# Expert down rows asked for by ScalarE on its own DMA queue, gate and up rows by the sync engine on the other

## The chip, the core and the metric

The kernel runs on one core of a Trainium2 chip. A core has five instruction streams: TensorE (PE, matmuls; its weight loads are shown apart as PEld), VectorE (DVE), ScalarE (ACT), GpSimd (POOL) and the sync engine (SP). Streams meet only at semaphores. Data come from device memory (HBM) by DMA: an instruction of one of the streams asks for a transfer, sixteen DMA engines carry it out, and a semaphore says that it has landed. The metric is the time on the device in microseconds (us).

## The reference, cut to what matters

The program is a two-layer decoder trunk. Each layer has three token mixers, a merge, an output projection and a channel mixer. The channel mixer of the second layer is a mixture of experts, and the change lies there alone:

```
logits = (tokens @ router_w)                       # 256 tokens, 8 experts
top_vals, top_idx = lax.top_k(logits, 2)
top_w = softmax(top_vals)
for e in range(8):                                 # w_gate, w_up: 1024 x 3584, w_down: 3584 x 1024
    y = (silu(tokens @ w_gate[e]) * (tokens @ w_up[e])) @ w_down[e]
    out = out + combine[:, e:e+1] * y
out = rmsnorm(x + out, final_norm_g)
```

All is float32, so that the eight experts are 352 MB of weights, each of which is read once in the run of the profile.

## The kernel before, in words

Everything up to line 1185 (both layers' mixers, the dense channel mixer, the routing) is the same in both kernels. Then comes the expert loop. Work is cut into passes: one pass takes one expert and up to 80 (CAP) of the tokens that chose it. The number of passes is found on the chip (`pass_expert`, a small table in SBUF, also says which expert each pass takes). The profile shows eight passes. A pass gathers its tokens into `xgT`, goes through four rounds (NR), and scatters the result into `x`.

A round covers 896 of the 3584 hidden columns, and needs 11 pieces of weights, each with a buffer of its own and no second one:

- eight "hidden" pieces (`hidden_slot(n)`, 128 x 2 x 896 floats): gate rows for even n, up rows for odd n;
- three "down" pieces (`down_slot(n)`): two of 128 x 2 x 1024 floats and one of 128 x 3 x 1024.

TensorE (L1217 to L1302) does in each round `hidden()`, which multiplies by the hidden pieces in order n = 0 to 7 and adds one to `hid_used` when it is through with each; then `down(0)`, which waits for down pieces 0 and 1 at its start, multiplies by them and adds one to `dwn_used`; then `down(1)`, which waits for piece 2, multiplies by it in two halves and adds one to `dwn_mm` after each. All three are the helper `columns_mm`, whose matmuls stand at L639; a round has 448 matmul records for the hidden part (56 for each piece) and 224 for the down part (128 in `down(0)`, 96 in `down(1)`). Between hidden and down, ScalarE takes Silu of the gate half in two parts (L1584, L1587) and VectorE multiplies by the up half (L2023, L2026). After round four, ScalarE copies the sums out of PSUM (`yT`, L1592), TensorE turns them (L1292), ScalarE copies them again (`ye`, L1596), TensorE scatters (L1298), turns the next pass's selection (L1210) and gathers its tokens.

The sync engine asks for all weights, in one queue (q1 in the trace). For each round it runs `later_round` (L2156): eight times "wait until TensorE is through with hidden piece n of the round before, ask for the next" (L2123), then down pieces 0 and 1 behind a wait on `dwn_used`, then piece 2 behind a wait on `dwn_mm` (L2128). Since it takes its instructions in order, the down pieces of a round always stand in the queue behind that round's hidden pieces, which is the order in which TensorE needs them. The last round of a pass asks for the first round of the next pass; two reads of `pass_expert` into a register (L2177, L2179) say from which expert. The first round's pieces of the first pass are asked for earlier, at L2138 to L2150, also by SP.

Of the kernel before, what the change touches and what calls it, by code (L numbers as in the profile page):

```python
# [9 lines left out]
ACT = mybir.ActivationFunctionType  # L10
AX_X = mybir.AxisListType.X

P = 128
# [12 lines left out]
FFD, FFE, NE = 2816, 3584, 8  # L26
# [4 lines left out]
CAP = 80  # L31
MAX_PASSES = 2 * T // CAP + NE
MIN_PASSES = -(-2 * T // CAP)
# [6 lines left out]
FB = 7  # L40
NR = FT // FB
SPLIT = 4
HSLOT = 2 * FB * P
KH = 4
# [23 lines left out]
def build(nc, a, out):  # L68
    ctx = ExitStack()
    with ctx:  # L70
        def sb(name, shape, dt=F32):
            return ctx.enter_context(nc.sbuf_tensor(name, shape, dt))

        def sem(name):
            return ctx.enter_context(nc.semaphore(name))
# [46 lines left out]
        def region(floats, at=None):  # L122
            start = top[0] if at is None else at
            assert start + floats <= ring_floats + arena_floats, (start, floats, ring_floats + arena_floats)
            top[0] = max(top[0], start + floats) if at is None else top[0]
            return pool[:, start:start + floats]
# [8 lines left out]
        def down_slot(n):  # L135

            lo = 2 * KH * HSLOT
            return pool[:, lo + 2 * n * D:lo + min(2 * n + (3 if n == 2 else 2), FB) * D].rearrange("p (f n) -> p f n", n=D)
# [4 lines left out]
        proj, B = banks[:2], banks[2:]  # L143
# [82 lines left out]
        sge = region(FB * CAP).rearrange("p (j n) -> p j n", j=FB)  # L226
# [10 lines left out]
        pass_expert = sb("pass_expert", [1, 32], I32)  # L237
# [14 lines left out]
        hid_loaded, dwn_loaded = slot_loaded[0:2 * KH], slot_loaded[2 * KH:2 * KH + 3]  # L252
        hid_used = sem("hidden_used")
        dwn_used = sem("down_used")
# [184 lines left out]
        he_silu, he_ready, hid_mm, dwn_mm = ff_silu.handle, ff_ready.handle, proj_mm.handle, down_mm.handle  # L439
# [31 lines left out]
        hid_base = DEPTH * proj_mm.per_layer  # L471
        ff_base = ff_ready.per_layer
        down_base = down_mm.per_layer

        block = ctx.enter_context(nc.Block())


        @block.gpsimd
        def _(gp):
# [846 lines left out]
        def _(act):  # L1326
# [8 lines left out]
            A = act.activation  # L1335

            def ln_exp_tables():

                act.preload_act_table_set("natural_log_exp_and_others")
# [237 lines left out]
            act.wait_ge(margin_ready, 1)  # L1577
            A(rs[:, 8:10], rs[:, 4:6], ACT.Exp).then_inc(marg_exp, 1)
            act.wait_ge(passes_ready, 1)
            n_pass = act.value_load(pass_expert[0:1, 0:1], min_val=MIN_PASSES, max_val=MAX_PASSES)  # L1580
            with act.Fori(0, n_pass) as i:
                for r in range(NR):
                    act.wait_ge(hid_mm, i * NR + (hid_base + r + 1))
                    A(sge[:, 0:SPLIT, :], B[2][:, 0:SPLIT * CAP].rearrange("p (f n) -> p f n", f=SPLIT),  # L1584
                      ACT.Silu).then_inc(he_silu, 1)
                    act.wait_ge(hid_used, i * (2 * KH * NR) + (2 * KH * (r + 1)))
                    A(sge[:, SPLIT:FB, :], proj[0][:, 0:(FB - SPLIT) * CAP].rearrange("p (f n) -> p f n", f=FB - SPLIT),  # L1587
                      ACT.Silu).then_inc(he_silu, 1)

                for half in range(2):  # L1590
                    act.wait_ge(dwn_mm, i * (2 * NR) + (down_base + 2 * NR - 1 + half))
                    A(yT[:, 4 * half:4 * half + 4, :], B[4 + half][:, 0:4 * CAP].rearrange("p (k n) -> p k n", k=4),  # L1592
                      ACT.Copy).then_inc(yT_ready, 1)
                for half in range(2):
                    act.wait_ge(ye_mm, i * 2 + (half + 1))
                    A(ye[0:CAP, half * 512:half * 512 + 512], B[2 + half][0:CAP, :], ACT.Copy).then_inc(ye_ready, 1)  # L1596
            ln_exp_tables()
            for t in range(NT):
                act.wait_ge(all_added, t + 1)
# [473 lines left out]
        def _(sp_):  # L2073
# [16 lines left out]
            def load(n):  # L2090

                src, _, s, _, former = loads[n]
                if former is not None:
                    sp_.wait_ge(*freed[former])
                if n == L[0]["ffn_first"]:
                    merge_step.wait(sp_, 0, 12)
                if n >= L[0]["ffn_first"] and former is None and (s + 1) * SLOT > mT_at:
                    xo_mm.wait(sp_, 0, 4)
                sp_.dma_start(weights(n), src).then_inc(slot_loaded[s], 16)
# [18 lines left out]
            def hidden_load(n, e, col):  # L2118

                w = (a["moe_w_gate"], a["moe_w_up"])[n % 2]  # L2120
                rows = slice(n // 2 * 2 * P, (n // 2 + 1) * 2 * P)
                src = w[0, e, rows, col].rearrange("a (k p) n -> p (a k) n", p=P)
                sp_.dma_start(hidden_slot(n), src).then_inc(hid_loaded[n], 16)  # L2123

            def down_load(n, e, rows):

                src = a["moe_w_down"][0, e, rows, :].rearrange("a (f p) n -> p (a f) n", p=P)
                sp_.dma_start(down_slot(n), src).then_inc(dwn_loaded[n], 16)  # L2128

            def down_rows(n):  # L2130
                return 2 * n * P, (3 if n == 2 else 2) * P


            oc_ready.wait(sp_, DEPTH - 1, 4)
            for n in range(RING, MRING):
# [1 line left out]
                    sp_.wait_ge(*freed[slot_last[n]])  # L2137
            for n in range(3):  # L2138
                lo, size = down_rows(n)
                down_load(n, slice(0, 1), slice(lo, lo + size))  # L2140
            clear, fetched = [], []
            for ring in [None] + sorted(range(RING), key=lambda n: slot_last[n]):
                if ring is not None:
# [9 lines left out]
            sp_.wait_ge(passes_ready, 1)  # L2153
            sp_.dma_start(fgain, a["final_norm_g"].partition_broadcast(P)).then_inc(fgain_loaded, 16)

            def later_round(e, col, hid, dwn):  # L2156

                for n in range(2 * KH):
                    sp_.wait_ge(hid_used, hid + (n + 1))
                    hidden_load(n, bass.ds(e, 1), bass.ds(col, FB * P))  # L2160
                for n in range(3):
                    if n < 2:
                        sp_.wait_ge(dwn_used, dwn + 1)
                    else:
                        sp_.wait_ge(dwn_mm, dwn * 2 + (down_base + 2))
                    lo, size = down_rows(n)
                    down_load(n, bass.ds(e, 1), bass.ds(col + lo, size))

            def rest_of_pass(i, e):

                with sp_.Fori(0, NR - 1) as j:
                    later_round(e, j * (FB * P) + FB * P, i * (2 * KH * NR) + j * (2 * KH), i * NR + j)

            more = sp_.value_load(pass_expert[0:1, MAX_PASSES + 1:MAX_PASSES + 2], min_val=MIN_PASSES - 1,
                                  max_val=MAX_PASSES - 1)
            with sp_.Fori(0, more) as i:
                e = sp_.value_load(pass_expert[0:1, bass.ds(i + 1, 1)], min_val=0, max_val=NE - 1)  # L2177
                rest_of_pass(i, e)
                e = sp_.value_load(pass_expert[0:1, bass.ds(i + 2, 1)], min_val=0, max_val=NE - 1)  # L2179
                later_round(e, 0, i * (2 * KH * NR) + (2 * KH * (NR - 1)), i * NR + (NR - 1))  # L2180
            e = sp_.value_load(pass_expert[0:1, bass.ds(more + 1, 1)], min_val=0, max_val=NE - 1)
            rest_of_pass(more, e)
            for t in range(NT):
                sp_.wait_ge(*((fin0_ready, 2), (fin_ready, 1))[t])
# [30 lines left out]
```

## Time and profile before

| | |
|---|---|
| median of 3 runs | 2028.77 us (2024.67 to 2029.76) |
| the profiled execution's own time | 2029.26 us |
| its span, first to last instruction | 2027.5 us |
| mean granted TensorE clock | 0.988 of full speed |
| busy: PE, PEld, DVE, ACT, POOL | 1951.6, 1729.5, 391.8, 273.1, 87.9 us |
| DMA | 482.99 MB |

The span is cut into 40 slices of 50.7 us in the page's second part. The expert loop fills the last 17 of them. A busy PE is not PE at its peak: the ends of matmuls are modelled, and short waits inside a merged run of matmuls may not show. "SPq" is the sync engine's own sequencer, and the duration of a DMA row there is the time that asking took, not the transfer's.

### The profile page before, as it was taken

What the parts mean: (1) busy time and instruction counts of PE and PEld (TensorE: products, weight loads), DVE (VectorE), ACT (ScalarE), POOL (GpSimd) and SP (SyncE); (2) the same over time, 40 slices, a digit from 0 to 9 for tenths busy, and PEclk for the clock granted to TensorE, in tenths of its full rate; (3) what the DMA queues carried; (4) which work ended last, traced back from release to release, by engine and by line L of the source; (5) the groups of instructions that cost most, each with busy time, mean ns of one, the idle gap of its engine ahead of it and who ended that gap; (6) DMA issues with size and microseconds to landing.
All of it is one profiled execution on the core that took longest, in us unless ns stands there. A gap on an engine that the chain in (4) does not pass through costs nothing.

```text
span 2027.5 us, 67804 instructions
## 1 busy us (share of the span) xinstructions
PE 1951.6 (96%) x31726; PEld 1729.5 (85%) x31726; DVE 391.8 (19%) x945; ACT 273.1 (13%) x580; POOL 87.9 (4%) x174
## 2 busy tenths in 40 slices
PE   7999999999999999999999799999999999999998
PEld 7888888888777688888888799999999898989897
DVE  3335331110000133533211301001010101010001
ACT  1323214000000122222310000000000000000001
POOL 4011101000000001011100000000000000000000
PEclk9999999999999999999999799999999999999999
DMA  7413123466443051320337299999999999999996
GB/s 243 125 45 103 44 85 104 146 221 236 145 145 104 22 167 43 104 65 23 125 125 251 102 380 407 407 407 407 407 407 407 407 407 407 407 407 407 407 407 267
DMA packets 214764, 482.99 MB, mean 238 GB/s; under 512 B 11582, under 2 KB 110092, under 8 KB 214668
## 3 DMA queue, kind: packets, MB, share of 16 engines
q1 hardware_dynamic: 214668, 481.54, 63.9%
q8 instruction: 81, 1.33, 0.3%
q14 instruction: 15, 0.12, 0.0%
HBM read 480.46 MB, written 1.05 MB: 237 GB/s over the span
## 4 chain that ended last, share of the span: by engine, by line
PE 84%; DMA 6%; SPq 4%; DVE 3%; ACT 1%; issue 1%; POOL 0%; DVEq 0%; ACTq 0%
PE bank L639 32%; PE bank L626 18%; PE bank L1154 7%; DMA pool<-in_moe_w_down_dram 6%; PE bank L723 5%; PE bank L1081 4%; PE bank L1114 4%; SPq L2123 3%; PE bank L1097 3%; PE bank L687 2%; PE bank L1298 1%; SPq L2128 1%; PE bank L1044 1%; DVE pool L1817 0%; PE bank L1004 0%
## 5 line engine op out<-in xcount | busy, mean ns | idle before, releaser
L639 PE MATMUL bank<-pool 128*64 128x80 f32 x21504 | 760.0, 234 | 31.7 <-DMA pool<-in_moe_w_down_dram 23.9
L639 PEld LDWEIGHTS bank<-pool 128*64 128x64 f32 x21504 | 754.0, 138 | 39.1 <-DMA pool<-in_moe_w_down_dram 26.0
L626 PE MATMUL bank<-hnT,pool 128*128 128x256 f32 x1856 | 427.7, 384 | 0.4 <-DVE pool L1879 0.4
L626 PEld LDWEIGHTS bank<-hnT,pool 128*128 128x128 f32 x1856 | 346.1, 190 | 55.1 <-issue 8.8
L1154 PEld LDWEIGHTS bank<-hnT,pool 128*128 128x128 f32 x640 | 121.6, 190 | 23.4 <-issue 7.7
L1154 PE MATMUL bank<-hnT,pool 128*128 128x256 f32 x640 | 140.7, 379 | 0.0
L2023 DVE TENSOR_TENSOR pool<-pool,bank 128x320 f32<-128x320 f32 x32 | 15.6, 488 | 638.4 <-ACT pool L1584 638.4
L723 PEld LDWEIGHTS bank<-pool 64*64 64x64 f32 x3008 | 94.8, 135 | 17.2 <-issue 11.3
L1584 ACT ACTIVATE pool<-bank 128x320 f32<-128x320 f32 x32 | 14.0, 437 | 690.1 <-PE bank L639 690.1
L723 PE MATMUL bank<-pool 64*64 64x32 f32 (+2 forms) x3008 | 103.4, 221 | 2.6 <-DVE pool L1663 1.6
L564 POOL TENSOR_TENSOR pool<-pool,level_mask 128x256 f32<-128x256 f32 x72 | 51.9, 735 | 773.8 <-DVE pool L1739 493.8
L1081 PE MATMUL bank<-oT,pool 128*128 128x256 f32 x384 | 85.4, 380 | 0.0
L1081 PEld LDWEIGHTS bank<-oT,pool 128*128 128x128 f32 x384 | 72.8, 190 | 10.2 <-issue 0.3
L1114 PE MATMUL bank<-pool 128*128 128x512 f32 x176 | 78.4, 593 | 0.0
L1114 PEld LDWEIGHTS bank<-pool 128*128 128x128 f32 x176 | 33.4, 190 | 35.0 <-issue 30.3
L1097 PE MATMUL bank<-pool 128*128 128x256 f32 x256 | 55.9, 379 | 0.0
L1097 PEld LDWEIGHTS bank<-pool 128*128 128x128 f32 x256 | 48.5, 190 | 6.5
L639 PE MATMUL bank<-hnT,pool 128*64 128x128 f32 x768 | 47.2, 288 | 3.5 <-DVE hnT L1634 3.5
L639 PEld LDWEIGHTS bank<-hnT,pool 128*64 128x64 f32 x768 | 45.8, 146 | 4.8 <-issue 4.8
L1913 DVE TENSOR_TENSOR pool<-pool,bank 128x256 f32<-128x256 f32 x22 | 9.3, 421 | 194.6 <-ACT pool L1562 194.6
L1663 DVE TENSOR_TENSOR pool<-pool,bank 128x128 f32<-128x128 f32 x108 | 26.7, 284 | 92.5 <-PE bank L723 92.5
L2035 DVE TENSOR_TENSOR x<-x,bank 128x512 f32<-128x512 f32 x32 | 22.0, 687 | 97.7 <-PE bank L1298 97.7
(324 smaller groups left out, 1188.4 us busy)
## 6 DMA issues: line engine op xcount, KB each, us to landing
pool<-in_moe_w_up_dram SPq DMA_DIRECT2D x128, 896.0 KB, 16.6
pool<-in_moe_w_gate_dram SPq DMA_DIRECT2D x128, 896.0 KB, 16.5
pool<-in_w_in_dram SPq DMA_DIRECT2D x66, 1024.0 KB, 5.4
pool<-in_moe_w_down_dram SPq DMA_DIRECT2D x64, 1024.0 KB, 16.6
pool<-in_moe_w_down_dram SPq DMA_DIRECT2D x32, 1536.0 KB, 18.6
pool<-in_ffn_w_gate_dram SPq DMA_DIRECT2D x11, 1024.0 KB, 7.6
pool<-in_ffn_w_up_dram SPq DMA_DIRECT2D x11, 1024.0 KB, 5.6
pool<-in_ffn_w_down_dram SPq DMA_DIRECT2D x11, 1024.0 KB, 5.1
```

Of the source, the lines that this page charges most:

```text
L564: ml_ready.by(gp.tensor_tensor(Ml[:, 4 * g:4 * g + 4, :], m_of(g), rep(level_mask[:, b, :], 4), ALU.mult))
L626: ins = mm(ps[:, s * T:(s + 1) * T], w[:, k, (j + s) * P:(j + s + 1) * P], hnT[:, k, :], start=(k == 0), stop=(k == KD - 1))
L639: ins = mm(bank[rows, cs], w[:, rows], rhs, start=start, stop=stop, skip_group_check=True)
L687: ins = mm(ps[:, half * SW:(half + 1) * SW], hnT[:, k, t * P:(t + 1) * P], weights(n)[:, k, :], start=(k == 0), stop=(k == KD - 1))
L723: ins = mm(out(rows), lhs(rows), rhs(rows), start=True, stop=True, skip_group_check=True)
L1081: ins = mm(ps[:, s * T:(s + 1) * T], weights(n)[:, k, (j0 + s) * P:(j0 + s + 1) * P], oT[:, m // 4, k, :], start=(k == 0), stop=(k == GH - 1))
L1097: ins = mm(bank[:, s * SW:(s + 1) * SW], mT[:, k, t * P:(t + 1) * P], weights(n)[:, k, :], start=(k == 0), stop=(k == KD - 1))
L1114: ins = mm(B[2 * t + half][:, :], ffT[:, f, t * P:(t + 1) * P], weights(n)[:, i, half * 512:half * 512 + 512], start=(f == 0), stop=(f == ...
L1154: ins = mm(proj[f % 2][:, s * T:(s + 1) * T], w[:, k, i * P:(i + 1) * P], hnT[:, k, :], start=(k == 0), stop=(k == KD - 1))
L1663: ins = tt(old, old, part(B[2 + g][:, k * T:(k + 1) * T]), ALU.subtract)
L2035: ins = tt(x[:, t, cs], x[:, t, cs], (B[0], B[1], proj[0], proj[1])[t + 2 * half][:, :], ALU.add)
L2123: sp_.dma_start(hidden_slot(n), src).then_inc(hid_loaded[n], 16)
```

## The change

The down pieces of all rounds but the very first are now asked for by ScalarE, whose requests go to another queue than SP's. `down_rows` and `down_load` move to the top of the block and take the queue as an argument. SP's `later_round` keeps the eight hidden pieces. ScalarE's loop, which ran over all passes, now runs over all but the last, as SP's did; it reads the expert's number into a register twice in a pass. In a pass it does: `hidden_round` (the two Silus), then `down_round` for the next round (the same waits, on `dwn_used` and `dwn_mm`, and the same three requests), three times; the fourth `hidden_round`; `outputs` (`yT`); the second read of the table; `rows_out` (`ye`); and only then `down_round` for the next pass's first round.

```
+            def down_round(e, row, used):
+                act.wait_ge(dwn_used, used + 1)
+                for n in range(3):
+                    if n == 2:
+                        act.wait_ge(dwn_mm, used * 2 + (down_base + 2))
+                    lo, size = down_rows(n)
+                    down_load(act, n, bass.ds(e, 1), slice(row + lo, row + lo + size))
...
+            def rounds(i, e):
+                for r in range(NR):
+                    hidden_round(i, r)
+                    if r < NR - 1:
+                        down_round(e, (r + 1) * (FB * P), i * NR + r)
+                outputs(i)
+
+            with act.Fori(0, more) as i:
+                e = act.value_load(pass_expert[0:1, bass.ds(i + 1, 1)], min_val=0, max_val=NE - 1)
+                rounds(i, e)
+                e = act.value_load(pass_expert[0:1, bass.ds(i + 2, 1)], min_val=0, max_val=NE - 1)
+                rows_out(i)
+                down_round(e, 0, i * NR + (NR - 1))
+            e = act.value_load(pass_expert[0:1, bass.ds(more + 1, 1)], min_val=0, max_val=NE - 1)
+            rounds(more, e)
+            rows_out(more)
...
-            def later_round(e, col, hid, dwn):
+            def later_round(e, col, hid):
                 for n in range(2 * KH):
                     sp_.wait_ge(hid_used, hid + (n + 1))
                     hidden_load(n, bass.ds(e, 1), bass.ds(col, FB * P))
-                for n in range(3):
-                    if n < 2:
-                        sp_.wait_ge(dwn_used, dwn + 1)
-                    else:
-                        sp_.wait_ge(dwn_mm, dwn * 2 + (down_base + 2))
-                    lo, size = down_rows(n)
-                    down_load(n, bass.ds(e, 1), bass.ds(col + lo, size))
```

ScalarE at the end of a pass, before. The first pair of rows is `yT`, the second `ye`, the last two close the loop:

```order
L1591 ISA
L1592 ACTIVATE pool<-bank 128x320 [waits down_mm]
L1591 REGISTER_ALU
L1592 ACTIVATE pool<-bank 128x320 [waits down_mm]
L1595 ISA
L1596 ACTIVATE hnT<-bank 80x512 [waits ye_mm]
L1595 REGISTER_ALU
L1596 ACTIVATE hnT<-bank 80x512 [waits ye_mm]
L1581 REGISTER_ALU
L1581 COMPARE_AND_BRANCH
```

Nothing stands between the copies and the next pass. The same place in the changed kernel, from the second `yT` copy on:

```order
L1613 ACTIVATE pool<-bank 128x320 [waits down_mm]
L1633 ISA
L1633 TENSOR_LOAD pass_expert
L1633 ISA x2
L1619 ISA
L1620 ACTIVATE hnT<-bank 80x512 [waits ye_mm]
L1619 REGISTER_ALU
L1620 ACTIVATE hnT<-bank 80x512 [waits ye_mm]
L1593 REGISTER_ALU
L484 ISA [waits down_used]
L484 DMA pool<-in_moe_w_down_dram 128x2x1024
L484 ISA
```

A read of the table now stands ahead of the `ye` copies, and the down requests of the next pass behind them. The sync engine in the second part of its pass loop, before, from the last hidden piece to the end of the pass:

```order
L2123 DMA pool<-in_moe_w_up_dram 128x2x896 [waits hidden_used]
L2163 ISA
L2128 DMA pool<-in_moe_w_down_dram 128x2x1024 [waits down_used]
L2128 ISA [waits down_used]
L2128 DMA pool<-in_moe_w_down_dram 128x2x1024
L2165 ISA
L2128 ISA [waits down_mm]
L2128 DMA pool<-in_moe_w_down_dram 128x3x1024
L2176 REGISTER_ALU
L2176 COMPARE_AND_BRANCH
```

The down requests stood right behind the last hidden request. The same place in the changed kernel:

```order
L2165 DMA pool<-in_moe_w_gate_dram 128x2x896
L2193 REGISTER_ALU
L2165 DMA pool<-in_moe_w_up_dram 128x2x896 [waits hidden_used]
L2203 REGISTER_ALU
L2203 COMPARE_AND_BRANCH
```

SP goes from the last hidden request straight to the next pass. The order on TensorE, VectorE and GpSimd is the same in both.

## Rows read from the trace of the kernel before

**Rows 1.** The page, span in 40 slices: TensorE, DMA share, GB/s

```profile
PE   7999999999999999999999799999999999999998
DMA  7413123466443051320337299999999999999996
GB/s 243 125 45 103 44 85 104 146 221 236 145 145 104 22 167 43 104 65 23 125 125 251 102 380 407 407 407 407 407 407 407 407 407 407 407 407 407 407 407 267
```

**Rows 2.** Windows: from:to, length, busy and count by engine, PEclk, DMA share, GB/s

```profile
1300.00:1400.00 100.00, 96.90 (x2635) 93.20 (x2632) 9.98 (x26) 6.57 (x13) 0.00 (x0) 1.00 1.03 407
...
1600.00:1700.00 100.00, 94.07 (x2541) 90.07 (x2539) 9.98 (x26) 6.57 (x13) 0.00 (x0) 1.00 1.03 407
...
2000.00:2027.50 27.50, 18.41 (x386) 15.33 (x386) 6.66 (x9) 7.99 (x14) 0.00 (x0) 0.95 0.38 150
```

**Rows 3.** The page, DMA issues: op xcount, KB each, us to landing

```profile
pool<-in_moe_w_up_dram SPq DMA_DIRECT2D x128, 896.0 KB, 16.6
...
pool<-in_moe_w_down_dram SPq DMA_DIRECT2D x64, 1024.0 KB, 16.6
pool<-in_moe_w_down_dram SPq DMA_DIRECT2D x32, 1536.0 KB, 18.6
```

**Rows 4.** DMA queues from 1200 to 2000 us: packets, MB, share

```profile
q1 hardware_dynamic: 92374, 325.78, 102.6%
q8 instruction: 1, 0.02, 0.0%
q14 instruction: 2, 0.02, 0.0%
```

**Rows 5.** TensorE's waits from 1200 us on: us in total, times, longest

```profile
PE bank L639 <- DMA pool<-in_moe_w_down_dram: 23.9, 13, 2.1
...
PE bank L639 <- DMA pool<-in_moe_w_up_dram: 3.9, 5, 0.9
```

**Rows 6.** Chain of waits: start us, us, what

```profile
1481.57 62.42 PE bank L639 x1792
```

**Rows 7.** Timeline at the end of a pass: start us, us, engine, line, operation

```profile
1445.72 6.12 SPq L2128 DMA_DIRECT2D pool<-in_moe_w_down_dram  x3
1452.98 2.72 SPq L2123 DMA_DIRECT2D pool<-in_moe_w_gate_dram  x1
...
1464.93 7.97 PE L639 MATMUL bank<-pool 128*64 128x80 f32 x224 [1.87 <-DMA pool<-in_moe_w_down_dram]
...
1472.28 6.81 SPq L2128 DMA_DIRECT2D pool<-in_moe_w_down_dram  x3
...
1472.94 0.44 ACT L1592 ACTIVATE pool<-bank 128x320 f32<-128x320 f32 x1 [1.22 <-PE bank L639]
...
1473.49 1.20 ACT L1596 ACTIVATE hnT<-bank 80x512 f32<-80x512 f32 x2
...
1481.57 28.66 PE L639 MATMUL bank<-pool 128*64 128x80 f32 x819
1485.08 0.38 SPq L2123 DMA_DIRECT2D pool<-in_moe_w_gate_dram  x1
```

**Rows 8.** Timeline of the last round on TensorE

```profile
2000.82 2.99 PE L639 MATMUL bank<-pool 128*64 128x80 f32 x80 [0.92 <-DMA pool<-in_moe_w_up_dram]
...
2005.94 7.97 PE L639 MATMUL bank<-pool 128*64 128x80 f32 x224 [2.13 <-DMA pool<-in_moe_w_down_dram]
```

**Rows 9.** DMA from 1990 to 2027.5 us in 40 slices of 0.94 us

```profile
GB/s 409 405 401 413 401 401 421 394 408 415 415 411 406 402 411 406 415 406 201 61 13 0 0 0 0 0 0 0 0 0 0 0 0 0 0 0 315 406 393 4
```

**Rows 10.** Line 2128 from 1200 us on: request ns min/median/max, landing

```profile
L2128 SPq DMA_DIRECT2D pool<-in_moe_w_down_dram x90: 372/1852/2755, 1209.9 to 1991.1; - x90
...
DMA to landing us min/median/max: 8.9/16.9/19.1
```

**Rows 11.** A request into an idle queue; then DMA from 1140 to 1160 us in slices of 0.5 us

```profile
1157.10 0.34 SPq L2154 DMA_DIRECT2D hnT<-in_final_norm_g_dram  x1
```

```profile
GB/s 409 409 444 409 409 445 409 409 409 172 0 0 0 0 0 0 0 0 0 0 0 0 0 0 0 0 0 0 0 0 0 0 0 0 0 0 180 401 295 123
```

More of the change, by code:

```diff
@@ L475, in build, with down_rows, down_load @@
         block = ctx.enter_context(nc.Block())
+        def down_rows(n):
+            return 2 * n * P, (3 if n == 2 else 2) * P
+        def down_load(queue, n, e, rows):
+            src = a["moe_w_down"][0, e, rows, :].rearrange("a (f p) n -> p (a f) n", p=P)
+            queue.dma_start(down_slot(n), src).then_inc(dwn_loaded[n], 16)
         @block.gpsimd
@@ L1579, in _, with hidden_round, outputs @@
             act.wait_ge(passes_ready, 1)
[L1580 to L1588, printed above, removed]
+            more = act.value_load(pass_expert[0:1, MAX_PASSES + 1:MAX_PASSES + 2], min_val=MIN_PASSES - 1,
+                                  max_val=MAX_PASSES - 1)
+            def down_round(e, row, used):
[5 more added lines that the diff above has]
+                    down_load(act, n, bass.ds(e, 1), slice(row + lo, row + lo + size))
+            def hidden_round(i, r):
+                act.wait_ge(hid_mm, i * NR + (hid_base + r + 1))
+                A(sge[:, 0:SPLIT, :], B[2][:, 0:SPLIT * CAP].rearrange("p (f n) -> p f n", f=SPLIT),
+                  ACT.Silu).then_inc(he_silu, 1)
+                act.wait_ge(hid_used, i * (2 * KH * NR) + (2 * KH * (r + 1)))
+                A(sge[:, SPLIT:FB, :], proj[0][:, 0:(FB - SPLIT) * CAP].rearrange("p (f n) -> p f n", f=FB - SPLIT),
+                  ACT.Silu).then_inc(he_silu, 1)
+            def outputs(i):
                 for half in range(2):
@@ L1593, in _, with rows_out @@
                       ACT.Copy).then_inc(yT_ready, 1)
+            def rows_out(i):
                 for half in range(2):
@@ L2123, in hidden_load @@
                 sp_.dma_start(hidden_slot(n), src).then_inc(hid_loaded[n], 16)
[L2125 to L2131, printed above, removed]
             oc_ready.wait(sp_, DEPTH - 1, 4)
@@ L2139, in _ @@
                 lo, size = down_rows(n)
-                down_load(n, slice(0, 1), slice(lo, lo + size))
+                down_load(sp_, n, slice(0, 1), slice(lo, lo + size))
             clear, fetched = [], []
@@ L2160, in later_round @@
                     hidden_load(n, bass.ds(e, 1), bass.ds(col, FB * P))
-                for n in range(3):
-                    if n < 2:
-                        sp_.wait_ge(dwn_used, dwn + 1)
-                    else:
-                        sp_.wait_ge(dwn_mm, dwn * 2 + (down_base + 2))
-                    lo, size = down_rows(n)
-                    down_load(n, bass.ds(e, 1), bass.ds(col + lo, size))
             def rest_of_pass(i, e):
                 with sp_.Fori(0, NR - 1) as j:
-                    later_round(e, j * (FB * P) + FB * P, i * (2 * KH * NR) + j * (2 * KH), i * NR + j)
+                    later_round(e, j * (FB * P) + FB * P, i * (2 * KH * NR) + j * (2 * KH))
             more = sp_.value_load(pass_expert[0:1, MAX_PASSES + 1:MAX_PASSES + 2], min_val=MIN_PASSES - 1,
@@ L2179, in _ @@
                 e = sp_.value_load(pass_expert[0:1, bass.ds(i + 2, 1)], min_val=0, max_val=NE - 1)
-                later_round(e, 0, i * (2 * KH * NR) + (2 * KH * (NR - 1)), i * NR + (NR - 1))
+                later_round(e, 0, i * (2 * KH * NR) + (2 * KH * (NR - 1)))
             e = sp_.value_load(pass_expert[0:1, bass.ds(more + 1, 1)], min_val=0, max_val=NE - 1)
```

## Prediction, made before the changed kernel ran

> **What bounds the kernel now.** I read the page's slices first, since the change lies in one stage. From the 25th slice to the 39th TensorE shows 9 in every slice and DMA shows 9 too, at 407 GB/s without a dip [rows 1]. Two engines can't both be the bound, so the windows come next. In them TensorE is busy 94 to 97 us of each 100, while the DMA share is 1.03 and the rate 407 GB/s whichever window is taken [rows 2]. Then the sizes: a round needs eight pieces of 896 KB, two of 1024 KB and one of 1536 KB [rows 3], which is 7.34 MB of hidden and 3.67 MB of down pieces, 11.01 MB in all. At 407 GB/s that is 27.05 us for a round and 108.2 us for a pass of four. TensorE alone would need less: 1792 matmuls without a stall take 62.42 us [rows 6], so a round of 672 takes 23.4 us, 15.6 for hidden and 7.8 for down; from the end of a pass's last matmul (1464.93 + 7.97 = 1472.9) to the next pass's start at 1481.57 [rows 7] go 8.7 us. A pass is thus 4 x 23.4 + 8.7 = 102.3 us of work on TensorE against 108.2 us of transfer. The loop is bound by transfers by 5.9 us a pass. The waits agree: those that show, 23.9 us for down pieces and 3.9 us for up pieces [rows 5], are on DMA; shorter ones are lost inside merged runs.
>
> So the loop ends when the last byte has come, plus what TensorE has yet to do with it. Three things can move the time: the rate, a stretch in which no transfer is asked for, and the order in which the last pieces land.
>
> **The change, part by part.** *Work removed and added on SP.* Three requests a round go. A down request takes SP 0.37 to 2.76 us [rows 10], the long ones while much is queued. SP waited on full queues and on TensorE, not the reverse, so this is worth 0; the cover is the queue itself, which is 16 to 18 us deep [rows 3].
>
> *Work added on ScalarE.* 31 of the 32 rounds' down requests, three each, up to 2.8 us apiece, 8.3 us at most. In the middle of a pass they stand between the end of `down(0)` and the next Silu, which comes 3.3 us of `down(1)` and 15.6 us of hidden work later. They fit, cost 0. At a pass's end the read of the table stands ahead of the `ye` copies, for which TensorE's scatter waits. The trace shows such a read only on SP, where the gap before the first request behind it is 1451.84 to 1452.98 [rows 7], 1.14 us with all else that lies in it. I take 1.1 us, seven times, with 0 and 1.1 as ends. It lengthens a pass on TensorE to 103.4 us, still under 108.2, so it costs nothing by itself; it counts below.
>
> *Order of the pieces.* Before, down pieces stood behind their round's hidden pieces. Now they are asked for in their own queue at t, the end of `down(0)`, when the same round's hidden pieces are still partly outstanding. How two deep queues share the engines no row of before shows, since all but three packets of 92,377 are on q1. The nearest rows are those three: packets of q8 and q14 landed inside stretches in which q1 had many us of work queued, and nothing on any engine stood still for that [rows 4]. That speaks for taking turns. Ends: the new queue gets nothing until the other is empty (as before), or goes wholly first. I take turns by halves.
>
> With halves, hidden pieces come late and TensorE waits for them instead of for down pieces. In the steady state: from the last hidden landing, TensorE needs 3.0 us to finish hidden (80 matmuls, rows 8, and the start of down there is held by nothing else) and 128/224 of 7.97 = 4.6 us for `down(0)`; landing is told up to some 2.3 us after the mean engine has moved its bytes (the second down piece landed at 2005.94 [rows 8] and 1.57 MB, 3.9 us, came behind it, while the bytes thin out at 2006.9 [rows 9], so 2.9 us at most). So t to t is h + 9.9 with h the time at which the hidden bytes are through. The period is still 27.05 us as long as the queues never run dry, so h = 17.15 us after t, in which 6.98 MB pass: 3.31 to 3.49 MB of hidden and the 3.67 MB of down, nearly all. **In the loop the stall only changes its name; cost 0.**
>
> *At the end* it does cost. Before, the last hidden piece landed at 2000.82 and the down pieces after it; TensorE's last run ended at 2005.94 + 7.97 = 2013.9 [rows 8], while bytes ended in the slice 2008.75 to 2009.7 [rows 9]: 4.4 us behind the last landing, at about 2009.5. With halves the hidden pieces land within 0.5 us of the last byte, and behind the last hidden piece stand 3.0 + 8.0 = 11.0 us. The same bytes end at the same time, so 11.0 - 4.4 = 6.6 us more, once. Ends: 0 if down pieces wait for hidden ones, 6.6 also if they go first.
>
> *At the seven pass boundaries* the queues come near to dry. Before, the last request was made at about 1477 and took up to 19.1 us to land [rows 7, 10], so at 1485.08, when the next request came, some 10 us were left. Now t = 1464.93 + 4.6 = 1469.5, and 3.3 to 3.5 MB of hidden are outstanding. ScalarE reaches its requests after `yT` (1473.38), the read (1474.5) and two `ye` copies (1475.7); a request into an idle queue started to move bytes 1.2 us later (1157.10 to 1158.3) [rows 11], thus at 1477, when the hidden rest lasts until 1477.6 or later. All 6.98 to 7.16 MB are through at 1486.6 to 1487.1. The next hidden request comes at 1485.08 + 1.1 and moves bytes from 1487.4. So 0.3 to 0.8 us run dry, each time; I take 0.6, seven times: 4.2 us. Ends: 0, and 2 us each (14 us) if requests come slower.
>
> The sum: 0 + 0 + 6.6 + 4.2 = 10.8 us, added to the profiled execution's 2029.26 gives 2040.1. The median of the runs shown lies 0.5 us under that execution, so I say 2039.5 us.
>
> *Against the skill.* The trace has one queue at 102.6% of sixteen engines' time [rows 4]. The Trainium skill (DMA: Bandwidth & Descriptors, Rules for kernel authors) says that spreading transfers over several issuing engines brings no bandwidth, since all use the same sixteen engines, and saves only time to issue; that speaks against a gain here, and the row leaves no idle share that would contradict it. Its section Queues, rings and completion order says that each DMA engine goes round the queues that have work, a packet from each; by that the sum is the one above, by arrival order it would be the first rival's. No row of before decides between them.
>
> **The rivals.** *Arrival order* (no change in effect, 0.2): if requests of both queues are served as they come, or the new queue gets a small share, the hidden pieces keep their place, since they are asked for before t. Last landing, tail and boundary stay: 2029, up to 2033 with a share of a third (h stays 17.15, 4.65 MB of hidden and 2.33 of down pass, 1.34 MB or 3.3 us remain behind the hidden pieces: 11.0 - 3.3 - 4.4 = 3.3 us). For it: SP asks for hidden pieces 16 us early. Against: the three packets above.
>
> *The rate rises* (0.17): two queues may overlap what one does in sequence between transfers. Each per cent is 8.2 us of the 820 us at 407 GB/s [rows 1]; 1 to 3% less the 10.8 us give 2015 to 2032. The floor is TensorE, 8 x 4.8 = 38 us less. For it: the slices of rows 9 and 11 go up to 421 and 445, though they also go down to 394. Against: the share is over 1.00 in every window, and 407 is the same to the digit [rows 2].
>
> *The rate falls* (0.08, slower by more): reads of two far regions of HBM in turn, or boundaries that run dry for 2 us. From 1% on it outweighs all else: 2029 + 6.6 + 8.2 + 4.2 = 2048, with 2% 2056. Nothing in the rows speaks for it, since q1 never had company.
>
> *ScalarE falls behind* (part of the last): should its requests block on a shared queue, 3 x 2.8 us still fit in 18.9 us, so only the boundary would show it.
>
> **How the numbers follow.** Turns by halves has 0.55, and by itself the range 2035 (no dry time: 2029.26 - 0.5 + 6.6) to 2046 (1.5 us dry at each boundary). The other cases widen it: below to 2020, which cuts off the rate from some 2.5% up, above to 2048, which cuts off most of the falling rate; some 0.1 is left out on each side. A measurement of this kernel can tell 0.3%, 6.1 us, from no change. Slower (over 2034.9): 0.50 of the first case and the falling rate's 0.08. Same: arrival order's 0.20, 0.05 of the first case, 0.03 of the rising rate. Faster: the other 0.14 of the rising rate.
>
> **What would show it.** Halves: after the change TensorE's waits name gate and up pieces and hardly down pieces; a down piece lands in 17 to 19 us still, a hidden piece later than 16.6; the last hidden piece lands within 1 us of the last byte, and from there to TensorE's last down matmul are 11 us instead of 4.4. Dry time: the rate at pass boundaries dips in slices of 1 us. The read: the gap between the last `yT` copy and the first `ye` copy grows from 0.1 to about 1.2 us. Wrong would be: waits still on down pieces (arrival order), a rate other than 407 between 1200 and 2000 us, or a dip of several us at each boundary.

## The result: 0.7% slower, and the profile after

The changed kernel took 2042.32 us (median of 4 runs, 2039.86 to 2045.13) against 2029.26 us of the kernel before measured beside it. The ratio is 1.0071, with a 95% interval of 1.0053 to 1.0090. The profiled execution is the fastest of the four, 2039.86 us with a span of 2038.1, 10.6 us longer than before.

The page's slices of the changed kernel, to be laid beside [rows 1]:

```profile
DMA  8413123476443151310436399999999999999995
GB/s 241 125 49 98 43 84 104 144 234 220 151 138 104 27 161 44 123 44 25 137 123 237 137 391 407 407 407 386 407 400 407 407 407 403 408 405 408 403 407 223
```

The loop still runs at 407 GB/s, but some slices now fall short (386, 400, 403, 405, 403). Before, none did. The DMA view from 1200 to 2000 us (packets, MB, share; then the requests with us to landing) says how much, beside [rows 4] and [rows 3]:

```profile
DMA packets 91790, 323.89 MB, mean 405 GB/s; under 512 B 5168, under 2 KB 5168, under 8 KB 91788
...
q1 hardware_dynamic: 64227, 216.67, 68.7%
q10 hardware_dynamic: 27561, 107.19, 33.7%
...
pool<-in_moe_w_up_dram SPq DMA_DIRECT2D x118, 896.0 KB, 14.2
...
pool<-in_moe_w_down_dram ACTq DMA_DIRECT2D x60, 1024.0 KB, 9.1
pool<-in_moe_w_down_dram ACTq DMA_DIRECT2D x30, 1536.0 KB, 17.3
```

323.89 MB where the kernel before moved 325.8: 1.9 MB less, 4.7 us of transfer at 407 GB/s. The big down pieces land 17.3 us after they are asked for, where it was 18.6, but the small ones after 9.1 instead of 16.7: they no longer stand behind anything. What they pass is the hidden pieces. TensorE's waits of the changed kernel, beside [rows 5]:

```profile
PE bank L647 <- DMA pool<-in_moe_w_up_dram: 28.1, 10, 3.7
...
PE bank L647 <- DMA pool<-in_moe_w_gate_dram: 4.3, 3, 2.7
```

No wait for a down piece is left among them. The sum is a little larger (32.4 us against 27.8), but the longest is 3.7 us instead of 2.1.

**The end.** The changed kernel's last round, beside [rows 8], and the DMA rate from 1990 to 2038.1 us in slices of 1.20 us, beside [rows 9]:

```profile
1993.02 3.70 ACTq L484 DMA_DIRECT2D pool<-in_moe_w_down_dram  x3
...
2012.52 11.98 PE L647 MATMUL bank<-pool 128*64 128x80 f32 x304 [3.54 <-DMA pool<-in_moe_w_up_dram]
```

```profile
GB/s 424 388 423 396 414 402 409 409 409 405 409 409 409 408 409 409 409 413 262 0 0 0 0 0 0 0 0 0 0 0 7 0 0 0 0 0 0 378 409 85
```

I count the end of the bytes by filling the last slices at 407 GB/s. Here that is 1990 + 18 x 1.20 + 262/407 x 1.20 = 2012.4; before it was 1990 + 18 x 0.94 + 275/407 x 0.94 = 2007.5 [rows 9]. TensorE's last down matmul ended at 2024.5 here and 2013.9 before [rows 8]. So the bytes end 4.9 us later, and TensorE is 12.1 us behind them instead of 6.4, 5.7 us more. Together 10.6 us, the difference of the spans.

**The clock.** The same 80 + 224 matmuls took 11.0 us before, in two runs, and 10.7 us in one run at the first pass end of the changed kernel. Windows of the changed kernel (PE, PEld, DVE, ACT, POOL, granted clock, DMA share, GB/s):

```profile
2009.00:2012.50 3.50, 0.00 (x0) 0.00 (x0) 0.00 (x0) 0.00 (x0) 0.00 (x0) 0.89 1.01 401
2012.50:2015.00 2.50, 2.48 (x38) 2.48 (x40) 0.00 (x0) 0.03 (x1) 0.00 (x0) 0.50 0.01 3
2015.00:2016.80 1.80, 1.80 (x55) 1.80 (x53) 0.49 (x1) 0.41 (x1) 0.00 (x0) 0.96 0.00 0
```

and one of the kernel before, after its wait of 0.9 us at the same place:

```profile
2000.80:2002.20 1.40, 1.38 (x40) 1.38 (x42) 0.00 (x0) 0.00 (x1) 0.00 (x0) 1.00 1.03 410
```

After idling for 3.5 us TensorE came back at 0.50, its lower level of 1.2 GHz, for 2.5 us. That is 1.25 us of the tail, 11.98 us against 10.73.

**A pass end.** The changed kernel's timeline, beside [rows 7], then its rate from 1475 to 1505 us in slices of 0.75 us:

```profile
1469.84 13.61 PE L647 MATMUL bank<-pool 128*64 128x80 f32 x304 [3.56 <-DMA pool<-in_moe_w_up_dram]
...
1483.50 0.44 ACT L1613 ACTIVATE pool<-bank 128x320 f32<-128x320 f32 x1 [1.22 <-PE bank L647]
...
1484.22 1.08 ACT L1620 ACTIVATE hnT<-bank 80x512 f32<-80x512 f32 x2 [0.29 <-PE bank L1300]
1484.87 1.53 ACTq L484 DMA_DIRECT2D pool<-in_moe_w_down_dram  x3
...
1492.30 17.93 PE L647 MATMUL bank<-pool 128*64 128x80 f32 x512
1495.82 0.38 SPq L2165 DMA_DIRECT2D pool<-in_moe_w_gate_dram  x1
```

```profile
GB/s 411 397 411 416 392 406 421 397 406 411 401 406 406 406 406 401 418 406 415 415 399 415 410 399 415 410 404 410 350 108 215 392 411 416 406 435 387 444 392 416
```

The rate falls to 108 in the slice that begins at 1496.75, about when the next hidden request, of 1495.82, starts to move bytes. The 304 matmuls took 13.6 us here, 2.9 more than the 10.7 at the full clock. The read of the table, for which I had up to 1.1 us, left 0.28 us between the last `yT` copy (end 1483.94) and the first `ye` copy, 0.2 more than before.

The seven pass ends are not alike. In the 40 us around each, in order, 0, 1.1, 0.4, 0, 0.2, 0.1 and 0.2 MB fewer are moved than at 407 GB/s. More than half of the loss lies at the second. There TensorE had waited twice (2.7 and 2.4 us, for pieces 6 and 7), and the rate fell twice, just before ScalarE's requests of 1375.87 moved bytes and again before the next hidden pieces did. The rate from 1360 to 1400 us in slices of 1 us:

```profile
GB/s 405 412 409 409 412 405 405 401 401 401 401 409 409 412 409 412 332 177 428 397 418 410 426 418 401 418 213 45 125 373 423 416 419 416 405 409 416 401 409 405
```

**How the queues share.** Packets, MB and share from 2000 to 2005 us in the changed kernel:

```profile
q10 hardware_dynamic: 283, 1.09, 55.0%
q1 hardware_dynamic: 281, 0.95, 48.0%
```

As many packets from one as from the other: they take turns. The down packets are longer, so they get somewhat over half of the bytes. In slices of 1 us this holds from 1997 on; the first bytes of the request made at 1993.02 moved only at about 1996.6.

### The profile page after: what moved, and what is told of

Its sections match the earlier page's. It is cut to its first block, busy times and chain, and to the rows that moved or that the text cites. A ratio compares the mean times of both kernels' runs of the same rounds, so it can differ in the third digit from the quotient of the medians.

```text
span 2038.1 us, 67871 instructions
## 1 busy us (share of the span) xinstructions
PE 1957.5 (96%) x31726; PEld 1736.4 (85%) x31726; DVE 391.8 (19%) x945; ACT 271.3 (13%) x580; POOL 88.2 (4%) x174
## 3 DMA queue, kind: packets, MB, share of 16 engines
q10 hardware_dynamic: 29264, 113.78, 14.1%
## 4 chain that ended last, share of the span: by engine, by line
PE 83%; DMA 11%; DVE 3%; ACT 1%; issue 1%; SPq 0%; ACTq 0%; POOL 0%; DVEq 0%
PE bank L647 32%; PE bank L634 18%; DMA pool<-in_moe_w_up_dram 11%; PE bank L1162 7%; PE bank L731 5%; PE bank L1089 4%; PE bank L1122 4%; PE bank L1105 3%; PE bank L695 2%; PE bank L1306 1%; PE bank L1052 1%; DVE pool L1859 0%; PE bank L1012 0%; PE bank L988 0%; PE bank L723 0%
## 5 line engine op out<-in xcount | busy, mean ns | idle before, releaser
L731 PEld LDWEIGHTS bank<-pool 64*64 64x64 f32 x3008 | 94.8, 135 | 17.3 <-issue 11.3
## 6 DMA issues: line engine op xcount, KB each, us to landing
pool<-in_moe_w_gate_dram SPq DMA_DIRECT2D x128, 896.0 KB, 11.3
```

Source lines behind the costliest of these rows:

```text
L731: ins = mm(out(rows), lhs(rows), rhs(rows), start=True, stop=True, skip_group_check=True)
```

## The experiments

I held three theories. *Order*: taking turns puts the last hidden piece of a round behind nearly all of its bytes, so that TensorE lags; that costs once at the end and where the lag lets the queues run dry. *A*: ScalarE's added reads and requests delay each pass. *B*: two queues move bytes more slowly. "Lost" below is 325.8 MB less what was moved from 1200 to 2000 us; "tail" is TensorE's last down matmul less the end of the bytes, counted as above, to some 0.1 us.

| kernel | ratio to before (95%) | lost, MB | tail, us |
|---|---|---|---|
| before | 1 | 0 | 6.4 |
| changed | 1.0071 (1.0053 to 1.0090) | 1.9 | 12.1 |
| last round's down on SP | 1.0033 (1.0020 to 1.0046) | 1.7 | 7.1 |
| pass end asked early | 1.0058 (1.0044 to 1.0071) | 1.9 | 13.8 |
| both of these | 1.0027 (1.0017 to 1.0037) | 1.5 | 7.1 |
| ScalarE's loop only | 0.9995 (0.9985 to 1.0004) | 0 | 6.5 |
| one queue, pieces 6 and 7 last | 1.0101 (1.0085 to 1.0117) | 5.2 | 11.6 |
| zeros in the wait | 1.0057 (1.0043 to 1.0072) | 0.8 | 14.1 |
| down requests held back | 1.0525 (1.0505 to 1.0545) | 34.9 | |
| fourth rounds' down on SP | 1.0035 (1.0022 to 1.0049) | 0 | 11.3 |
| fourth rounds and last pass on SP | 0.9994 (0.9985 to 1.0003) | 0 | 6.6 |

**ScalarE's loop only.** From the changed kernel, without requests on ScalarE; SP asks as before.

```
             def rounds(i, e):
                 for r in range(NR):
                     hidden_round(i, r)
-                    if r < NR - 1:
-                        down_round(e, (r + 1) * (FB * P), i * NR + r)
                 outputs(i)
...
                 rows_out(i)
-                down_round(e, 0, i * NR + (NR - 1))
```

> ScalarE has the changed kernel's loop, with the same reads of the table at the same places, but asks for nothing; the sync engine asks for all pieces in the order of before. Theory: the reads are covered by the transfers, 2029 as before, within 2 us. Rival A (ScalarE's reads ahead of the ye copies cost): up to 1.1 us in each of seven passes would show, and if they are the whole cause, 2042. Rival B: 2029.

Measured 2028.36 us, 0.9995. The reads and the new loop are free, which leaves of A only the requests.

**The last round's down pieces on SP.**

```
-            rest_of_pass(more, e)
+            with sp_.Fori(0, NR - 2) as j:
+                later_round(e, j * (FB * P) + FB * P, more * (2 * KH * NR) + j * (2 * KH))
+            later_round(e, (NR - 1) * (FB * P), more * (2 * KH * NR) + (NR - 2) * (2 * KH))
+            used = more * NR + (NR - 2)
+            for n in range(3):
+                if n < 2:
+                    sp_.wait_ge(dwn_used, used + 1)
+                else:
+                    sp_.wait_ge(dwn_mm, used * 2 + (down_base + 2))
+                lo, size = down_rows(n)
+                down_load(sp_, n, bass.ds(e, 1), slice((NR - 1) * (FB * P) + lo, (NR - 1) * (FB * P) + lo + size))
...
-            rounds(more, e)
+            rounds(more, e, NR - 2)
```

> Only the very last round's three down pieces go back to the sync engine's queue, behind that round's hidden pieces; the other 30 rounds' requests stay on ScalarE. Theory (order of the pieces costs once, at the end; plus dry queues at pass boundaries): the last hidden piece lands some 8 us ahead of the last byte, the run of 80 + 224 matmuls behind it no longer stands behind the last byte, and the time falls by 5 to 7 us from the changed kernel's 2042.3, to about 2036.5. Rival A (ScalarE's reads and requests delay the work of every pass): no change, 2042. Rival B (two queues move bytes more slowly all through the loop): one round in 31 less, 2042.

Measured 2034.12 us, 1.0033: about half of the loss is gone, by moving one round of 31. The gain of 8.2 us on the changed kernel's median is somewhat over the 5 to 7 expected; the trace shows 5 of it in the tail. TensorE's last run and the rate from 1990 to 2040 us in slices of 1.25:

```profile
1984.82 31.00 PE L647 MATMUL bank<-pool 128*64 128x80 f32 x888
...
2015.76 1.24 PE L1300 MATMUL bank<-ident,pool 128*80 128x128 f32 x8
```

```profile
GB/s 407 407 404 410 407 401 404 408 419 410 410 403 406 416 387 13 0 0 0 0 0 0 0 0 0 0 0 0 125 397 318 0 7 7 0 0 0 0 0 0
```

TensorE no longer waits for a last piece, and its work ends 7.1 us behind the bytes. The theories A and B had 2042. The 1.7 MB lost stay.

**Pass end asked early.** Down pieces 0 and 1 of the next pass are asked for ahead of the `yT` copies.

```
-            def down_round(e, row, used):
+            def down_round(e, row, used, pieces=range(3)):
...
-                rounds(i, e)
+                for r in range(NR):
+                    hidden_round(i, r)
+                    if r < NR - 1:
+                        down_round(e, (r + 1) * (FB * P), i * NR + r)
                 e = act.value_load(pass_expert[0:1, bass.ds(i + 2, 1)], min_val=0, max_val=NE - 1)
+                down_round(e, 0, i * NR + (NR - 1), range(2))
+                outputs(i)
                 rows_out(i)
-                down_round(e, 0, i * NR + (NR - 1))
+                down_round(e, 0, i * NR + (NR - 1), range(2, 3))
```

> At the end of a pass ScalarE asks for down pieces 0 and 1 of the next pass as soon as down(0) is through, ahead of the yT copies; piece 2 stays behind the ye copies, and all else is as changed. Theory: the dry stretches at the pass boundaries, 1.9 MB or 4.6 us between 1200 and 2000 us in the changed kernel's trace, shrink to under 1 us; time 3 to 5 us under 2042.3, about 2038.5. No slice of 1 us at a boundary under 380 GB/s. Rival A (ScalarE's own work is what costs): not faster, since the same work now stands ahead of the yT copies, 2042 to 2046. Rival B (a lower rate throughout): 2042.

Measured 2040.67 us, 1.0058; the interval overlaps the changed kernel's. The trace decides:

```profile
DMA packets 91800, 323.92 MB, mean 405 GB/s; under 512 B 5168, under 2 KB 5168, under 8 KB 91798
```

The same 1.9 MB are lost. (The longer tail in the table is the clock: the last 304 matmuls took 13.4 us instead of 12.0.) My expectation was wrong, and my own prediction had the reason: the queues run dry when *all* outstanding bytes are through. Asking earlier for the same bytes doesn't make them more. At the second pass end the rate now falls once instead of twice, and 1.0 MB are lost there instead of 1.1. What counts is when TensorE frees the next hidden buffer.

**Both edits**, the last round's and the pass end's, together.

> Both edits at once: last round's down pieces on the sync engine, and at pass ends pieces 0 and 1 asked for ahead of the yT copies. Theory: the two costs are separate and add, so both gains come: 2042.3 - 6 - 4 = about 2032, within 0.3% of the kernel before. If only one of the two gains shows, 2036 to 2039. Rivals A and B: 2042.

Measured 2034.11 us, 1.0027, between the 2032 expected with both gains and the 2036 to 2039 with one. It is the time of the first edit alone, 2034.12, and the intervals overlap; 1.5 MB are still lost. So the second edit shows no gain here either.

**One queue, pieces 6 and 7 last.** From the kernel before.

```
-                for n in range(2 * KH):
+                for n in range(2 * KH - 2):
                     sp_.wait_ge(hid_used, hid + (n + 1))
                     hidden_load(n, bass.ds(e, 1), bass.ds(col, FB * P))
                 for n in range(3):
...
+                for n in range(2 * KH - 2, 2 * KH):
+                    sp_.wait_ge(hid_used, hid + (n + 1))
+                    hidden_load(n, bass.ds(e, 1), bass.ds(col, FB * P))
```

> The kernel before, with one queue and nothing on ScalarE, but in every later round the sync engine asks for hidden pieces 6 and 7 behind the three down pieces instead of ahead of them. This brings about on one queue what two queues do by taking turns: the last hidden piece comes after nearly all of the round's bytes. Theory (order alone makes the loss): TensorE's waits name pieces 6 and 7, are over 3 us long, the tail behind the last byte is 11 to 12 us instead of 6.4, and pass ends run dry; 2038 to 2045. Rivals A and B (ScalarE's requests, or the second queue as such): 2029, no change.

Measured 2048.48 us, 1.0101, more than I expected. Rate and waits:

```profile
DMA packets 90868, 320.65 MB, mean 401 GB/s; under 512 B 5121, under 2 KB 5121, under 8 KB 90866
```

```profile
PE bank L639 <- DMA pool<-in_moe_w_gate_dram: 26.7, 14, 2.3
PE bank L639 <- DMA pool<-in_moe_w_up_dram: 13.7, 17, 0.9
```

```profile
2026.33 10.73 PE L639 MATMUL bank<-pool 128*64 128x80 f32 x304 [0.91 <-DMA pool<-in_moe_w_up_dram]
```

Two of the signs come on one queue with ScalarE untouched: waits on the last hidden pieces, in two steps of up to 2.3 and 0.9 us instead of one over 3, and 304 matmuls behind the last landing. For these, order alone is enough. The lost bytes are another matter. At each of the seven pass ends TensorE's 304 matmuls took 10.7 us and the rate held; it fell some 28 us later, in the new pass's first round, here in slices of 2.5 us from 1200 to 1300 us:

```profile
GB/s 407 404 404 408 403 404 408 413 410 408 404 404 410 406 406 404 411 404 415 411 402 410 406 404 407 405 404 412 405 413 406 408 407 404 404 410 407 400 238 129
```

SP had made a request at 1289.03, and its next, for the down pieces, came at 1297.52; pieces 6 and 7 had to stand behind it. That is the later asking that this edit brings with it, not the dry pass end of the changed kernel, so that the 5.2 MB don't count for the theory. The pass ends are settled by the fourth-round kernel below.

**Zeros in the wait.** From the changed kernel; the sums don't change.

```
                             slot_tiles(n, 0)
+                            for _ in range(4):
+                                mm(B[4][:, 0:4 * CAP], zeros[:, 0:P], zeros[:, :], start=False, stop=False,
+                                   skip_group_check=True)
                             hidden_arrived(n + 1)
```

> The changed kernel, but in each round TensorE does four matmuls with zeros (128 x 320 bf16, some 0.9 us in all) just before it waits for hidden piece 7, so that its idle stretch there is some 2.6 us instead of 3.5. They add zero to the sums. Theory: it is the stretch of 3.5 us that halves TensorE's clock for the 2 to 5 us behind it (304 matmuls in 12.0 to 13.6 us instead of 11.0), and this lag is what empties the queues at pass ends: the clock stays at 1.00, the 304 matmuls take 11 us, bytes lost to dry stretches fall from 1.9 MB to under 1 MB, time 2036 to 2040. Rival: the clock falls just the same behind 2.6 us, or the dry stretches don't come from the lag: 2042, or up to 2 us more in each pass for the added matmuls where TensorE has no slack.

Measured 2039.44 us, 1.0057, which its interval does not part from the changed kernel. The trace has less lost:

```profile
DMA packets 92108, 325.01 MB, mean 406 GB/s; under 512 B 5198, under 2 KB 5198, under 8 KB 92106
```

and the pass ends' 304 matmuls took 10.7, 12.2, 10.7, 10.8, 10.8, 12.4 and 10.7 us, where the changed kernel had 10.8, 13.4, 13.6, 12.1, 12.2, 12.4 and 13.4. So the clock fell less often and less was lost, as the theory says. The two ends of 12.2 and 12.4 us are also the two that lost bytes, 0.5 and 0.3 MB; the other five lost none. That the time follows is not shown. In the last round the clock fell all the same (304 in 12.4 us), and one piece landed 1.8 us behind the end of the bytes as I count it, so the tail is no shorter.

**Down requests held back.** From the changed kernel.

```
                     if r < NR - 1:
+                        act.wait_ge(hid_used, i * (2 * KH * NR) + (2 * KH * (r + 1) + 2))
                         down_round(e, (r + 1) * (FB * P), i * NR + r)
```

> The changed kernel, but inside a pass ScalarE first waits until TensorE is through with hidden piece 1 of the next round (some 7 us longer) before it asks for the down pieces. Two queues, the same requests, the same instructions on ScalarE but for three waits a pass. Theory: the hidden rest of 3.3 MB is nearly through when the down pieces come, TensorE waits for down pieces again, and never 3.5 us at a time; the last hidden piece lands 6 us or more ahead of the last byte, so the tail is that of before, and the queues don't run dry at the pass ends because TensorE no longer lags: 2028 to 2033. If dry stretches at pass ends come from the late requests there instead, they stay or grow: 2034 to 2038. Rivals A (ScalarE's work) and B (two queues are slower): 2042, and A somewhat more.

Measured 2137.04 us, 1.0525: all theories missed by 100 us. ScalarE's requests and TensorE's runs in two rounds of one pass:

```profile
1468.74 1.69 ACTq L484 DMA_DIRECT2D pool<-in_moe_w_down_dram  x3
...
1483.04 6.29 PE L647 MATMUL bank<-pool 128*64 128x80 f32 x128 [2.92 <-DMA pool<-in_moe_w_down_dram]
1490.36 19.14 PE L647 MATMUL bank<-pool 128*64 128x80 f32 x544 [1.03 <-DMA pool<-in_moe_w_down_dram]
...
1498.12 1.61 ACTq L484 DMA_DIRECT2D pool<-in_moe_w_down_dram  x3
```

Here a round is a closed chain: the request, 21.6 us until TensorE has down piece 2 (it shares the engines with the next hidden pieces), 3.4 us for `down(1)`, 3.9 us for hidden pieces 0 and 1, and the next request. That is 28.9 of the 29.4 us between the two requests, more than the 27.05 of the bytes, and through the last two parts down buffers stand empty and unasked for. At a pass's end it is worse. From the request of 1404.26 to the next, 1439.36, went 35.1 us: 7.4 until TensorE began the new pass, and 27.3 of its work up to hidden piece 1 of the second round, without a wait in it. That interval alone is 8 us over the bytes, of the 12.2 us by which this pass was longer than 108.2. I had counted what the order would do, not how long the chain would be. The run tells nothing between the theories.

**The fourth rounds' down pieces on SP**, in all passes.

```
-                with sp_.Fori(0, NR - 1) as j:
+                with sp_.Fori(0, NR - 2) as j:
                     later_round(e, j * (FB * P) + FB * P, i * (2 * KH * NR) + j * (2 * KH))
+                later_round(e, (NR - 1) * (FB * P), i * (2 * KH * NR) + (NR - 2) * (2 * KH))
+                used = i * NR + (NR - 2)
+                for n in range(3):
...
-                    if r < NR - 1:
+                    if r < NR - 2:
                         down_round(e, (r + 1) * (FB * P), i * NR + r)
```

The lines left out are the two waits and the request, as in the edit of the last round.

> In every pass, the down pieces of the fourth round alone are asked for by the sync engine behind that round's hidden pieces, as before; those of the other three rounds stay on ScalarE, the next pass's first ones at the same late place behind the ye copies. Theory: what empties the queues at a pass end is that TensorE comes out of the fourth round late (it has waited for that round's last hidden piece, 3.5 us and then at half clock), not when the next pass's pieces are asked for. So the dry stretches go, under 0.5 MB lost between 1200 and 2000 us instead of 1.9, and the tail is that of before: 2028 to 2031. If the late requests at the pass end, or the taking of turns in the other rounds, empty the queues, the 1.5 to 1.9 MB stay lost and only the tail is won: 2034, as with the last round alone. Rival B (two queues move bytes more slowly): 2039 or more, since three rounds in four still use both.

Measured 2033.29 us, 1.0035. Half of the expectation came. The MB from 1200 to 2000 us, and the rate from 1475 to 1505 us, beside the changed kernel's with its 108:

```profile
DMA packets 92351, 325.79 MB, mean 407 GB/s; under 512 B 5209, under 2 KB 5209, under 8 KB 92348
```

```profile
GB/s 406 397 421 397 410 410 401 407 416 399 404 421 404 407 412 409 406 410 410 411 408 404 410 404 415 399 408 397 411 411 401 401 406 411 397 411 411 397 411 416
```

Nothing is lost, though the next pass's pieces are asked for as late as in the changed kernel, and three rounds in four take turns. That the lag of the fourth round empties the queues is thus shown, and B is refuted. The time left over is in the last pass:

```profile
1981.84 36.08 PE L647 MATMUL bank<-pool 128*64 128x80 f32 x976 [3.66 <-DMA pool<-in_moe_w_up_dram]
2017.85 1.24 PE L1300 MATMUL bank<-ident,pool 128*80 128x128 f32 x8
```

TensorE waited 3.7 us for the *third* round's last hidden piece and then had 976 matmuls in a row, one and a half rounds, to the end. The bytes ended at 2006.6, 11.3 us before it was done.

**The last pass on SP as well.** To test that, all later rounds of the last pass go back to SP.

```
-            rounds(more, e)
+            rounds(more, e, 0)
```

> As the kernel with the fourth round's down pieces on the sync engine, and in the last pass all later rounds' down pieces there too, in the order of before. ScalarE still asks for those of rounds 1 to 3 in the first seven passes. Theory: in the kernel with the fourth round alone the queues never ran dry, but TensorE waited 3.7 us for the third round's last hidden piece and was then 11.3 us of work behind the last byte. With no such wait in the last pass it is at most 7 us behind; nothing else is lost, so 2028 to 2031, no slower than before by more than 0.1%. If taking turns in the first seven passes costs something that neither the dry stretches nor the tail shows, 2033 stays.

Measured 2029.07 us, 0.9994 (0.9985 to 1.0003), with 73.4 MB still on q10:

```profile
2000.48 2.99 PE L647 MATMUL bank<-pool 128*64 128x80 f32 x80 [0.93 <-DMA pool<-in_moe_w_up_dram]
2005.60 7.97 PE L647 MATMUL bank<-pool 128*64 128x80 f32 x224 [2.13 <-DMA pool<-in_moe_w_down_dram]
```

The last round is [rows 8] again. With ten of the 31 rounds' requests back on SP and 21 still on ScalarE, the whole loss is gone.

## Why the prediction was right

- *What bounds the loop* and that SP's lighter load is worth 0: held. Down requests take ScalarE 0.38 us in the median. That A's remaining part, the requests, costs nothing is shown by the last experiment, which makes most of them.
- *Turns by halves*: held, in the number of packets. The steady state came as worked out: waits moved from down to the last hidden piece. That piece's bytes were through some 18.4 us after the request, against the 17.15 of the working; q10's first bytes came 3.6 us after the request instead of 1.2, which was measured into an idle queue.
- *The end*, 6.6 us: 5.7 by the end of the bytes, of which some 1.2 us is the halved clock, which I had not foreseen; so the step itself was some 2 us too large. The 11.0 us behind the last byte were right (12.1 less the clock's 1.2); the 4.4 us of the kernel before were not. I had put the end of its bytes at 2009.5, where the last few packets fall; by the count used here it is 2007.5, 6.4 us ahead of TensorE's end. The fourth-round kernel sharpens it: what counts is TensorE's lag behind the last byte, and an earlier round's wait can cause it as well as the last round's.
- *Pass ends*, 4.2 us: 4.7 to 4.9 measured, but the step's account was partly wrong. It gave each of seven ends 0.6 us, with ScalarE's late requests and the table read in the chain. In fact the read costs 0.2 us and the time of the requests nothing in the sum; TensorE's lag out of the fourth round, made longer where the clock was halved, does it. Nor is it seven times 0.6 us: one end lost 2.7 us, one 1.0, three 0.3 to 0.5 and two nothing. The balance of outstanding bytes, the other half of the step, was near; that the total came within 1 us of the forecast is luck in part.
- *The sum*: 10.8 predicted, 10.6 between the spans, 13.1 between the medians. The profiled execution was the fastest of its four, and no trace shows the other 2.5 us.
- *The rivals*: arrival order is refuted by the packet counts, a changed rate by 325.79 MB with three rounds in four on two queues. The Trainium skill's rule that queues take turns packet by packet (DMA: Bandwidth & Descriptors, Queues, rings and completion order) agrees with the trace's 283 packets against 281; so does its rule that more issuing engines bring no bandwidth (the same page, Rules for kernel authors): 407 GB/s with one queue and with two.

## What to carry to other kernels

Where one queue already fills the DMA engines, the order of its requests is the schedule. A second queue brings no bytes, but takes the order away: it halves the rate of what is needed first in favour of what is needed later. The cost shows only where the consumer's lag can't be made up, at the end and wherever requests depend on it; so look at how much work is left behind the last byte, and at how many bytes are outstanding when the consumer pauses, and not at the sum of the waits.

## What the runs showed of the hardware that was not expected

- The clock's fall doesn't go by the length of the last wait alone. In the changed kernel waits of 3.4 to 3.7 us left TensorE at a granted clock of 0.50 for the next 2.5 us and more (304 matmuls in 12.0 to 13.6 us), but one of 3.4 us, at the first pass end, left it at 1.00 (10.7 us). In the kernel before a wait of 2.13 us in the last round left it at 1.00, and 224 matmuls took 7.97 us; one of 2.14 us left it at 0.50, and they took 9.55. Both stood behind a wait of 0.92 us and 80 matmuls. With zeros in the wait, 304 matmuls took 10.7 us behind a wait of 3.0 us and 12.4 behind one of 2.2. So the step of that experiment's expectation that a shorter wait keeps the clock is not borne out as a rule. The changed kernel behind its 3.4 us, and the kernel before behind its 2.14 us:

```profile
1252.00:1254.50 2.50, 2.47 (x70) 2.47 (x72) 0.49 (x1) 0.44 (x1) 0.00 (x0) 1.00 1.04 410
...
1789.55 9.55 PE L639 MATMUL bank<-pool 128*64 128x80 f32 x224 [2.14 <-DMA pool<-in_moe_w_down_dram]
...
1789.50:1792.00 2.50, 2.45 (x37) 2.46 (x38) 0.00 (x0) 0.00 (x0) 0.00 (x0) 0.50 1.02 408
```

- With q1 deeply filled, the first bytes of a request on q10 moved some 3.6 us after it was made (1993.02 to 1996.6); then the two queues took turns at once.
